# Moving the adaLN units of a three-block transformer kernel: openings of feed-forward groups, mixers that make their own gates, loads queued by free buffer

## The chip, the cores and the metric

One core of a Trainium2 chip runs the whole program. The metric is the device time of one execution in microseconds (us). TensorE (PE) multiplies, VectorE (DVE) and ScalarE (ACT) do the elementwise work, SyncE (SP) issues nearly all weight loads from one queue that is worked off in order, and GpSimd (POOL) issues a few small loads.

## The reference, cut to what matters

A sequence of 256 tokens of width 1024 passes nine sub-layers. Block 1 has two layers of feed-forward, mixer, feed-forward, each adapted by a vector c:

```python
cs = jax.nn.silu(c)
for l in range(2):
    mod = (cs @ ada_w[l] + ada_b[l]).reshape(B, 3, 3, 1024)[:, :, :, None, :]
    h = _rmsnorm(x, norm_g[l, 0]) * (1.0 + mod[:, 0, 1]) + mod[:, 0, 0]
    x = x + 0.5 * mod[:, 0, 2] * _swiglu(h, gate, up, down)
    h = _rmsnorm(x, norm_g[l, 1]) * (1.0 + mod[:, 1, 1]) + mod[:, 1, 0]
    x = x + mod[:, 1, 2] * _mixer(h, ...)
    h = _rmsnorm(x, norm_g[l, 2]) * (1.0 + mod[:, 2, 1]) + mod[:, 2, 0]
    x = x + 0.5 * mod[:, 2, 2] * _swiglu(h, gate, up, down)
return _rmsnorm(x, final_g)
```

Block 2 is one layer of feed-forward, mixer, feed-forward with norms and no adaption. The feed-forward is 2816 wide. Everything is float32.

## The kernel before

**Stages.** The nine sub-layers are stages s = 0 to 8: feed-forward, mixer, feed-forward, twice; then the same of block 2. The stage reads the normalised input `nh`/`nl` (an exact split of float32 into two parts) and ends in `change`, which adds the result to `x`, normalises it for the next stage and turns it on PE.

**Weight units.** Every weight arrives as a unit of 128 x 2048 float32 (1 MB). SP's `load(n)` puts unit n into buffer n % 3 of `raw`, after the unit three before it has been split (`lo_done`). ACT's `split` copies the unit to `hi` (rounded), DVE's `split` subtracts to get `lo` (L944), and PE multiplies three times with them. A split may start when PE is done with the unit that held the same `hi`/`lo` place: in a feed-forward four units earlier, in a mixer three. The fourth place is called `w`.

**Feed-forward.** 11 groups i = 0 to 10 of 256 hidden columns and three units each: `up(i, 0)` and `up(i, 1)` (gate and up weights, two loads for each unit) and `down(i)`. In group i PE does both halves of `up(i)` with the turning of the hidden tile of group i-1 between them, then `down(i-1)`, for which DVE's `low(i-1)` (L1086) must be done. DVE does in group i: split of `up(i+1, 0)`, `low(i-1)`, split of `up(i+1, 1)`, `mult(i)` (L1081), split of `down(i)`.

**Mixer of block 1.** Six value units (b+0 to b+5), twelve query and key units (b+6 to b+17), then four steps of three convolution units each with attention between them. Before the first of these steps PE waits until all three of its units, b+18 to b+20, are split (`arrive(c + 2)`). Then comes a tail of 18 units.

**adaLN units.** `mod` of a phase p (one phase for each of the first six stages) is 12 units of 1 MB: units 0 to 7 make scale and shift, units 8 to 11 the gate. A unit goes into `raw[:, 3]`, the one adaLN buffer, and DVE makes 256 columns of `acc` from it: `ada` is one multiply (L954) and seven multiply-adds (L957). SP's `load_ada` waits until the unit before it is used (`ada_used`); while it waits, everything behind it on SP's queue waits too. Scale and shift of phase p are due at the end of stage p-1 (`mods`), the gate of phase p in the middle of stage p (`gate_sums` on PE, `gates_in` on DVE). `ffn_ada` says which units stand behind the second `up` split of a group, ahead of `mult` (`mid`), and which behind its last split (`end`). The units stand so:

| stage | adaLN units before | after the change |
|---|---|---|
| 0 (feed-forward) | 16: phase 0 units 8 to 11, phase 1 all | 12: phase 0 units 8 to 11, phase 1 units 0 to 7 |
| 1 (mixer) | 12: phase 2 | 16: phase 1 units 8 to 11, phase 2 all |
| 2 (feed-forward) | 12: phase 3 | 9: phase 3 units 0 to 8 |
| 3 (feed-forward) | 12: phase 4 | 11: phase 3 units 9 to 11, phase 4 units 0 to 7 |
| 4 (mixer) | 12: phase 5 | 16: phase 4 units 8 to 11, phase 5 all |

In both mixers six of the units stand in the tail and do not change; the other six (before) or ten (after) stand ahead of it.

Of the kernel before, what the change touches and what calls it, by code (L numbers as in the profile page):

```python
# [43 lines left out]
NG = FF // UC  # L44
# [8 lines left out]
BASE = [sum(UNITS[k] for k in STAGES[:s]) for s in range(len(STAGES))]  # L53
# [23 lines left out]
def down_unit(i):  # L77

    return 3 * i + 4 if i < NG - 1 else 3 * NG - 1
# [32 lines left out]

def ffn_ada(s):

    if s == 0:
        units, twice = [(0, u) for u in range(8, 12)] + [(1, u) for u in range(12)], (1, 2, 3, 4, 5, 6)
    elif s in (2, 3):
        units, twice = [(s + 1, u) for u in range(12)], (3, 6)
    else:
        return [None] * NG, [None] * NG  # L120
    units = iter(units)
    mid, end = [None] * NG, [None] * NG
    for i in range(NG - 1):
        mid[i] = next(units) if i in twice else None
        end[i] = next(units)
    return mid, end


def stat_events():
# [21 lines left out]
def build(nc, a, out):  # L151
    ctx = ExitStack()
    with ctx:
# [240 lines left out]
        def _(sp):  # L394
# [13 lines left out]
            def load_ada(unit):  # L408

                if unit is None:  # L410
                    return
                p, u = unit
                n = ada_no(p, u)
                if n:
                    sp.wait_ge(ada_used, n)
                else:
                    sp.wait_ge(ada_p, 4)
                sp.dma_start(raw[:, 3, :].rearrange("p (k f) -> p k f", k=KC),
                             ada_v[p // 3][:, :, (p % 3) * 3 * D + u * UC:(p % 3) * 3 * D + (u + 1) * UC])\
                    .then_inc(raw_full[3], 16)  # L420

            def ffn(s, g_v, u_v, d_v):
                b = BASE[s]
                mid, end = ffn_ada(s)

                def up(i, kh):
                    rows_, c = slice(4 * kh, 4 * kh + 4), slice(i * UC, (i + 1) * UC)
                    load(b + up_unit(i, kh), g_v[:, rows_, c], u_v[:, rows_, c])

                up(0, 0)  # L430
                up(0, 1)
                up(1, 0)
                up(1, 1)
                load(b + down_unit(0), d_v[0])
                for i in range(NG):
                    load_ada(mid[i])
                    if i + 2 < NG:
                        up(i + 2, 0)
                        up(i + 2, 1)
                    elif i + 2 == NG:  # L440
                        load(b + down_unit(NG - 1), d_v[NG - 1])
                    load_ada(end[i])
                    if i + 2 < NG:
                        load(b + down_unit(i + 1), d_v[i + 1])

            def tail(s, at, units, srcs, wo, ada):
                for n, (kind, j) in enumerate(units):
# [7 lines left out]
            def mixer(s, l):  # L455
                b = BASE[s]
                for n in range(6):
                    e = n % 2
                    load(b + n, win_v[l][:, 4 * e:4 * e + 4, 2 * QKV + n // 2 * 512:2 * QKV + (n // 2 + 1) * 512])
                load_ada((s + 1, 0))  # L460
                for n in range(12):
                    c = n % 2 * QKV + n // 2 * UC
                    if n >= 6 and n % 2 == 0:
                        load_ada((s + 1, n // 2 - 2))
                    load(b + 6 + n, win_v[l][:, :, c:c + UC])
                for n in range(12):
                    if n in (0, 2):
                        load_ada((s + 1, 4 + n // 2))
                    c = 3 * QKV + n % 3 * D + n // 3 * UC
                    load(b + 18 + n, win_v[l][:, :, c:c + UC])  # L470
                tail(s, TAIL_AT1, TAIL1,
                     {"ga": (win_v[l], 3 * QKV + 4 * D, UC), "ya": (wao_v[l], 0, 512),
                      "gc": (win_v[l], 3 * QKV + 3 * D, UC), "yc": (wco_v[l], 0, UC)}, wo_v[l], s + 1)
# [464 lines left out]
        def _(dve):  # L938
# [21 lines left out]
            def ada(unit):  # L960
                if unit is not None:
                    ada_unit(unit[1] * UC, 3, (ada_no(*unit) + 3) * 16, ada_used)
# [87 lines left out]
                    dve.drain()  # L1050
                    V.tensor_tensor(xh, xh, f1[:, :], ALU.add).then_inc(x_done, 1)

            def change(s, early, between, behind):

                Aq = s + 1
                for t in range(2):
                    if t == 0:
                        early()
                    if s < 6:
                        add_gated(s, t)  # L1060
                    else:
                        add_postnorm(s, t)
                    if s == 5:
                        final_norm(t)
                    if s < 8:
                        normed(Aq, t)
                        if t == 0:
                            between()
                            if Aq < 6:
                                mods(Aq)  # L1070
                        apply(Aq, t)
                if s < 8:
                    behind()

            def ffn(s, fo, first=None):
                b = BASE[s]
# [20 lines left out]
                mult(0, 0)  # L1097
                mult(0, 1)
                split(b + 4)
                ada(end[0])  # L1100
                for i in range(1, NG - 1):
                    split(b + 3 * i + 2)
                    low(i - 1)
                    split(b + 3 * i + 3)
                    ada(mid[i])
                    mult(i, 0)
                    mult(i, 1)
                    if i == 6 and s < 6:
                        gates_in(s)
                    split(b + 3 * i + 4)  # L1110
                    ada(end[i])
                split(b + 32)
                low(NG - 2)
                if s < 8:
# [144 lines left out]
            def mixer(s, l):  # L1259
                b = BASE[s]  # L1260
                V.tensor_copy(cwl[:, :], vec[:, l * 24 + V_CONV:l * 24 + V_CONV + 24])
                for n in range(6):
                    split(b + n + 3)
                for r in range(6):
                    if r == 3:
                        gates_in(s)
                    split(b + 9 + 2 * r)
                    split(b + 10 + 2 * r)
                    ada((s + 1, r))
                st0 = l * STEPS  # L1270

                def conv(j, taps):
# [57 lines left out]
            def ffn_change(s, late, behind):  # L1330

                if s < 6:
                    def between():
                        late()
                        split(BASE[s + 1] + 1)
                    change(s, nothing, between, behind)
                elif s < 8:
                    def early():
                        late()
                        split(BASE[s + 1] + 1)  # L1340
                    change(s, early, nothing, behind)
                else:
                    change(s, late, nothing, nothing)

            def wo_change(s, behind):

                def between():
                    split(BASE[s + 1])
                    split(BASE[s + 1] + 1)
                change(s, nothing, between, behind)  # L1350

            for l in range(DEPTH):
                s = 3 * l
# [519 lines left out]
```

## Time and profile before

| | |
|---|---|
| median of 3 runs | 2357.85 us (2356.15 to 2358.1) |
| the profiled execution: its time, its span | 2358.23 us, 2355.8 us |
| PE busy | 2144.4 us, 91% of the span |
| DVE busy | 1428.8 us, 61% |
| ACT busy | 1008.7 us, 43% |
| read from memory | 435.05 MB, 185 GB/s over the span |

PE is the engine that is nearly always busy, so the time outside of its work is what can be won. Its idle time is the span less its busy time, 211.4 us. Where a row below has a bracket, it says how long the engine sat idle before that instruction and which engine's result ended the idle time. PEclk is the clock that TensorE was granted, as a share of full speed.

### The profile page before, as it was taken

The page shows a single profiled execution, that of the slowest core. Times are in us where ns is not written, and L with a number is a line of the kernel's source. Part 1 is how long each engine was busy: PE and PEld are TensorE (multiplying, and loading weights), DVE is VectorE, ACT ScalarE, POOL GpSimd, SP SyncE. Part 2 cuts the span into 40 slices and gives each one's busy share as a digit, 9 for nine tenths or more (in the row PEclk, how much of TensorE's full clock was granted, in tenths as well). Part 3 has the DMA queues.
Part 4 walks back from the last instruction along what each step waited for, and adds up shares of the span by engine and source line. Part 5 has one row for each costly group of instructions (what it writes and reads, how often), then busy time and mean ns, then how long its engine had stood idle before and what let it go on. Part 6 is the DMA issues. An engine that isn't in the chain of part 4 may idle for free.

```text
span 2355.8 us, 29867 instructions
## 1 busy us (share of the span) xinstructions
PE 2144.4 (91%) x12059; PEld 1860.6 (79%) x12059; DVE 1428.8 (61%) x1885; ACT 1008.7 (43%) x1249; POOL 31.3 (1%) x57
## 2 busy tenths in 40 slices
PE   6889996899989998999959999999899887799998
PEld 5677796799867776778959998887788776797887
DVE  3677645567766676766446686545544557656554
ACT  2433442443443353335324445434544546645433
POOL 0000000000000000000000000000000000000000
PEclk9999999899999999999989999999999898899999
DMA  7687565556657747766465575654555432254662
GB/s 231 222 267 247 183 210 174 154 154 203 232 171 252 249 158 245 247 227 190 159 196 136 153 253 167 213 191 146 182 193 182 140 119 72 74 193 156 213 193 90
DMA packets 355917, 438.10 MB, mean 186 GB/s; under 512 B 9563, under 2 KB 323355, under 8 KB 355780
## 3 DMA queue, kind: packets, MB, share of 16 engines
q1 hardware_dynamic: 350592, 420.51, 54.5%
q0 software_dynamic: 4160, 14.23, 2.7%
q8 instruction: 96, 1.57, 0.3%
q10 hardware_dynamic: 1028, 1.45, 0.2%
q14 instruction: 41, 0.34, 0.0%
HBM read 435.05 MB, written 1.11 MB: 185 GB/s over the span
## 4 chain that ended last, share of the span: by engine, by line
PE 54%; DVE 20%; DMA 15%; ACT 6%; issue 3%; DVEq 2%; SPq 1%; ACTq 0%
DMA raw<-in_ada_w 11%; DVE acc L957 8%; DVE lo L944 6%; PE PC L1467 4%; PE PC L1468 4%; PE PC L1469 4%; PE PA L1467 4%; PE PA L1469 4%; PE PA L1468 4%; PE PA L1460 3%; DMA raw<-in_w_in 3%; PE PA L1461 3%; PE PA L1462 3%; PE PB L1467 3%; PE PB L1469 3%; PE PB L1468 3%
## 5 line engine op out<-in xcount | busy, mean ns | idle before, releaser
L944 DVE TENSOR_TENSOR lo<-raw,hi 128x2048 fp32r<-128x2048 f32 x277 | 633.6, 2288 | 345.1 <-ACT hi L584 344.6
L584 ACT ACTIVATE hi<-raw 128x2048 fp32r<-128x2048 f32 x277 | 528.8, 1910 | 403.8 <-PE PC L1469 190.4
L1460 PE MATMUL PA<-nl,hi 128*128 128x256 f32 x976 | 291.7, 299 | 53.9 <-DVE lo L944 53.9
L1461 PE MATMUL PA<-nh,lo 128*128 128x256 f32 x976 | 284.0, 291 | 0.0
L1462 PE MATMUL PA<-nh,hi 128*128 128x256 f32 x976 | 283.2, 290 | 0.0
L957 DVE SCALAR_TENSOR_TENSOR acc<-raw,cs,acc 128x256 f32<-128x256 f32 x476 | 230.7, 485 | 36.9 <-issue 1.4
L1460 PEld LDWEIGHTS PA<-nl,hi 128*128 128x128 f32 x976 | 195.8, 201 | 56.8 <-issue 42.9
L1467 PE MATMUL PA<-hi,nl 128*128 128x512 f32 (+1 forms) x528 | 212.7, 403 | 16.2 <-DVE nl L1016 9.9
L1469 PE MATMUL PA<-hi,nh 128*128 128x512 f32 (+1 forms) x528 | 208.4, 395 | 0.0
L1468 PE MATMUL PA<-lo,nh 128*128 128x512 f32 (+1 forms) x528 | 208.1, 394 | 0.0
L1467 PE MATMUL PC<-hi,cL 128*128 128x512 f32 x384 | 160.2, 417 | 49.4 <-DVE cL L1086 44.8
L1461 PEld LDWEIGHTS PA<-nh,lo 128*128 128x128 f32 x976 | 195.7, 200 | 0.7 <-issue 0.5
L1462 PEld LDWEIGHTS PA<-nh,hi 128*128 128x128 f32 x976 | 195.3, 200 | 0.0
L1467 PE MATMUL PB<-hi,nl 128*128 128x512 f32 x400 | 158.3, 396 | 5.8 <-DVE gate_b L980 2.8
L1468 PE MATMUL PC<-lo,cH 128*128 128x512 f32 x384 | 157.0, 409 | 0.0
L1469 PE MATMUL PC<-hi,cH 128*128 128x512 f32 x384 | 156.4, 407 | 0.0
L1469 PE MATMUL PB<-hi,nh 128*128 128x512 f32 x400 | 156.1, 390 | 0.0
L1468 PE MATMUL PB<-lo,nh 128*128 128x512 f32 x400 | 155.8, 389 | 0.0
L944 DVE TENSOR_TENSOR w<-raw,w 128x2048 fp32r<-128x2048 f32 x51 | 116.6, 2287 | 36.7 <-ACT w L584 36.7
L1467 PEld LDWEIGHTS PC<-hi,cL 128*128 128x128 f32 x384 | 76.7, 200 | 75.2 <-DVE lo L944 45.0
L1467 PEld LDWEIGHTS PA<-hi,nl 128*128 128x128 f32 x528 | 102.9, 195 | 38.2 <-issue 19.1
L584 ACT ACTIVATE w<-raw 128x2048 fp32r<-128x2048 f32 x51 | 97.5, 1912 | 62.1 <-PE PC L1469 50.2
(281 smaller groups left out, 3902.4 us busy)
## 6 DMA issues: line engine op xcount, KB each, us to landing
raw<-in_w_in SPq DMA_DIRECT2D x90, 1024.0 KB, 7.2
raw<-in_ada_w SPq DMA_DIRECT2D x72, 1024.0 KB, 5.6
raw<-in_ffn_w_gate SPq DMA_DIRECT2D x88, 512.0 KB, 4.1
raw<-in_ffn_w_up SPq DMA_DIRECT2D x88, 512.0 KB, 5.3
raw<-in_ffn_w_down SPq DMA_DIRECT2D x44, 1024.0 KB, 5.6
raw<-in_ffn_w SPq DMA_DIRECT2D x88, 512.0 KB, 4.8
raw<-in_ffn_w SPq DMA_DIRECT2D x22, 1024.0 KB, 4.9
raw<-in_w_o SPq DMA_DIRECT2D x12, 1024.0 KB, 5.1
```

The lines of the kernel that those rows point to most:

```text
L584: A(parts_of(n)[0], raw[:, n % 3, :], ACT.Copy).then_inc(hi_done, 1)
L944: V.tensor_tensor(l, raw[:, n % 3, :], h.bitcast(F32), ALU.subtract).then_inc(lo_done, 1)
L957: i = V.scalar_tensor_tensor(o, w[:, k, :], cs[:, k:k + 1], o, ALU.mult, ALU.add)
L1460: MM(o, wh[:, c0:c0 + w], xl, start=first, stop=False, skip_group_check=True)
L1461: MM(o, wl[:, c0:c0 + w], xh, start=False, stop=False, skip_group_check=True)
L1462: return MM(o, wh[:, c0:c0 + w], xh, start=False, stop=last, skip_group_check=True)
L1467: MM(o, xl, wh[:, c0:c0 + w], start=first, stop=False, skip_group_check=True)
L1468: MM(o, xh, wl[:, c0:c0 + w], start=False, stop=False, skip_group_check=True)
L1469: return MM(o, xh, wh[:, c0:c0 + w], start=False, stop=last, skip_group_check=True)
```

## The change

Three things are changed at once. First, in a feed-forward the adaLN unit of group i is the first thing that DVE does in it (`ada(mid[i])`, groups 1 to 9), and the second units (`end`), of which there are three in stage 0 (groups 4, 6, 8), none in stage 2 and two in stage 3 (groups 4, 6), stand between `mult(i)` and the split of `down(i)`. Second, each mixer of block 1 makes the four gate units of its own phase, so it has ten units ahead of its tail, each behind one split. Third, SP's queue has its adaLN loads at other points: in a feed-forward behind the load of `up(i + 2, 0)`, and for the unit after a second one behind the load of `down(i + 1)`; in a mixer behind the load of b+3, and then each behind the weight load that waits for the same split as the adaLN unit before it. Besides, `low_tile` of the last hidden tile is done right after `add_gated` of the first token tile (stages 0, 2, 3, 5), and in stage 6 behind the split that it stood ahead of.

```diff
 def ffn_ada(s):
-    if s == 0:
-        units, twice = [(0, u) for u in range(8, 12)] + [(1, u) for u in range(12)], (1, 2, 3, 4, 5, 6)
-    elif s in (2, 3):
-        units, twice = [(s + 1, u) for u in range(12)], (3, 6)
-    else:
+    phases = {0: (0, 8, 1, 8), 2: (3, 0, 3, 9), 3: (3, 9, 4, 8)}
+    if s not in phases:
         return [None] * NG, [None] * NG
+    p0, u0, p1, u1 = phases[s]
+    units = [(p0, u) for u in range(u0, 12 if p1 > p0 else u1)] + [(p1, u) for u in range(u1 if p1 > p0 else 0)]
+    twice = (4, 6, 8)[:len(units) - 9]
...
+    for i in range(1, NG - 1):
+        mid[i] = next(units)
+        end[i] = next(units) if i in twice else None
+MIX_ADA = (1, 3, 5, 6, 8, 10, 11, 13, 15, 17)
+def mix_ada(s):
+    return [(s, u) for u in range(8, 12)] + [(s + 1, u) for u in range(6)]
 # SP, feed-forward
-                for i in range(NG):
-                    load_ada(mid[i])
-                    if i + 2 < NG:
-                        up(i + 2, 0)
-                        up(i + 2, 1)
-                    elif i + 2 == NG:
-                        load(b + down_unit(NG - 1), d_v[NG - 1])
-                    load_ada(end[i])
-                    if i + 2 < NG:
-                        load(b + down_unit(i + 1), d_v[i + 1])
+                for i in range(NG - 2):
+                    up(i + 2, 0)
+                    load_ada(end[i] or mid[i + 1])
+                    up(i + 2, 1)
+                    load(b + down_unit(i + 1), d_v[i + 1])
+                    if end[i]:
+                        load_ada(mid[i + 1])
+                load(b + down_unit(NG - 1), d_v[NG - 1])
 # SP, mixer
-                load_ada((s + 1, 0))
+                    if n == 3:
+                        load_ada(mix_ada(s)[0])
                 for n in range(12):
-                    if n >= 6 and n % 2 == 0:
-                        load_ada((s + 1, n // 2 - 2))
                     load(b + 6 + n, win_v[l][:, :, c:c + UC])
+                    if n in MIX_ADA:
+                        load_ada(mix_ada(s)[MIX_ADA.index(n) + 1])
                 for n in range(12):
-                    if n in (0, 2):
-                        load_ada((s + 1, 4 + n // 2))
                     load(b + 18 + n, win_v[l][:, :, c:c + UC])
+                    if n + 12 in MIX_ADA[:-1]:
+                        load_ada(mix_ada(s)[MIX_ADA.index(n + 12) + 1])
 # DVE, change
                         add_postnorm(s, t)
+                    if t == 0:
+                        midway()
 # DVE, feed-forward
-                ada(end[0])
                 for i in range(1, NG - 1):
+                    ada(mid[i])
                     split(b + 3 * i + 2)
                     low(i - 1)
                     split(b + 3 * i + 3)
-                    ada(mid[i])
                     mult(i, 0)
                     mult(i, 1)
                     if i == 6 and s < 6:
                         gates_in(s)
+                    ada(end[i])
                     split(b + 3 * i + 4)
-                    ada(end[i])
 # DVE, mixer
-                for n in range(6):
+                for n in range(18):
+                    if n == 12:
+                        gates_in(s)
                     split(b + n + 3)
-                for r in range(6):
-                    if r == 3:
-                        gates_in(s)
-                    split(b + 9 + 2 * r)
-                    split(b + 10 + 2 * r)
-                    ada((s + 1, r))
+                    if n in MIX_ADA:
+                        ada(mix_ada(s)[MIX_ADA.index(n)])
 # DVE, ffn_change (late is low_tile of the last hidden tile)
                 if s < 6:
-                    def between():
-                        late()
-                        split(BASE[s + 1] + 1)
-                    change(s, nothing, between, behind)
+                    change(s, nothing, late, lambda: split(BASE[s + 1] + 1), behind)
                 elif s < 8:
                     def early():
+                        split(BASE[s + 1] + 1)
                         late()
-                        split(BASE[s + 1] + 1)
-                    change(s, early, nothing, behind)
+                    change(s, early, nothing, nothing, behind)
```

## Rows read from the trace of the kernel before

**Rows 1.** The page: the chain that ended last, by engine.
```profile
PE 54%; DVE 20%; DMA 15%; ACT 6%; issue 3%; DVEq 2%; SPq 1%; ACTq 0%
```

**Rows 2.** Windows: busy us of PE, PEld, DVE, ACT, POOL; PEclk, DMA share, GB/s.
```profile
96.00:101.00 5.00, 4.97 (x12) 3.96 (x13) 4.38 (x6) 0.00 (x0) 0.00 (x0) 0.52 1.08 354
...
330.00:421.00 91.00, 63.85 (x504) 62.08 (x502) 45.41 (x54) 27.87 (x23) 0.00 (x0) 0.89 0.57 182
```

**Rows 3.** Timeline of PE, stages 1 and 4: start us, us, instruction, idle before.
```profile
370.26 0.38 PE L1460 MATMUL PC<-nl,hi 128*128 128x256 f32 x1 [1.69 <-DVE lo L944]
...
421.24 0.55 PE L1460 MATMUL PA<-nl,hi 128*128 128x256 f32 x1 [21.08 <-DVE lo L944]
...
1223.95 0.55 PE L1460 MATMUL PA<-nl,hi 128*128 128x256 f32 x1 [20.96 <-DVE lo L944]
```

**Rows 4.** Timelines of SP, ACT and DVE, one period of stage 1.
```profile
374.41 0.37 SPq L418 DMA_DIRECT2D raw<-in_ada_w  x1
374.82 1.89 SPq L406 DMA_DIRECT2D raw<-in_w_in  x2
...
382.60 1.91 ACT L584 ACTIVATE hi<-raw 128x2048 fp32r<-128x2048 f32 x1 [11.32 <-DMA raw<-in_w_in]
...
384.55 2.29 DVE L944 TENSOR_TENSOR lo<-raw,hi 128x2048 fp32r<-128x2048 f32 x1 [6.76 <-ACT hi L584]
387.18 3.84 DVE L957 SCALAR_TENSOR_TENSOR acc<-raw,cs,acc 128x256 f32<-128x256 f32 x7
```

**Rows 5.** Timeline of ACT: evictions of query and key units, PE never idle.
```profile
326.59 0.60 ACT L812 ACTIVATE q<-PA 128x512 f32<-128x512 f32 x1 [2.87 <-PE PA L1462]
...
332.35 0.60 ACT L810 ACTIVATE k<-PA 128x512 f32<-128x512 f32 x1 [3.37 <-PE PA L1462]
```

**Rows 6.** Timeline of DVE, stage 6: `low` of two groups with no adaLN unit.
```profile
1713.37 0.69 DVE L1086 TENSOR_TENSOR cL<-PA,cH 128x512 fp32r<-128x512 f32 x1 [2.38 <-ACT cH L671]
...
1730.23 0.69 DVE L1086 TENSOR_TENSOR cL<-PB,cH 128x512 fp32r<-128x512 f32 x1 [2.40 <-ACT cH L671]
```

**Rows 7.** Timelines of SP and DVE: first burst of stage 2; of stage 3.
```profile
664.46 0.37 SPq L406 DMA_DIRECT2D raw<-in_ffn_w_gate  x1
...
667.62 0.51 SPq L418 DMA_DIRECT2D raw<-in_ada_w  x1
...
676.48 0.35 DVE L954 TENSOR_SCALAR acc<-raw,cs 128x256 f32<-128x256 f32 x1 [6.98 <-DMA raw<-in_ada_w]
...
880.61 0.37 SPq L406 DMA_DIRECT2D raw<-in_ffn_w_gate  x1
```

**Rows 8.** Timeline of ACT, stage 2: the second `up` unit of that burst.
```profile
673.48 1.92 ACT L584 ACTIVATE hi<-raw 128x2048 fp32r<-128x2048 f32 x1 [1.20 <-DMA raw<-in_ffn_w_up]
```

**Rows 9.** Timelines of SP and DVE, stage 0: an adaLN load with little ahead of it.
```profile
93.11 0.37 SPq L418 DMA_DIRECT2D raw<-in_ada_w  x1
...
98.36 0.35 DVE L954 TENSOR_SCALAR acc<-raw,cs 128x256 f32<-128x256 f32 x1 [0.28 <-DMA raw<-in_ada_w]
```

**Rows 10.** PE: first `down`, gate sums, ninth `down` of stage 0; ninth, stages 2, 3.
```profile
96.03 0.77 PE L1467 MATMUL PC<-hi,cL 128*128 128x512 f32 x1 [7.59 <-DVE cL L1086]
...
194.18 1.98 PE L1519 MATMUL PB<-acc,ones_w 128*128 128x512 f32 x4 [3.03 <-DVE cL L1086]
...
250.05 0.47 PE L1467 MATMUL PC<-hi,cL 128*128 128x512 f32 x1 [2.03 <-DVE cL L1086]
...
832.51 0.47 PE L1467 MATMUL PC<-hi,cL 128*128 128x512 f32 x1 [0.99 <-DVE cL L1086]
...
1051.74 0.47 PE L1467 MATMUL PC<-hi,cL 128*128 128x512 f32 x1 [1.84 <-DVE cL L1086]
```

**Rows 11.** Timelines of DVE and PE at the end of stage 5.
```profile
1651.74 1.13 DVE L1008 TENSOR_SCALAR ub_b<-PC,vec 128x128 f32<-128x128 f32 x4 [4.09 <-PE PC L1529]
...
1645.60 0.77 PE L1467 MATMUL PC<-hi,cL 128*128 128x512 f32 x1 [4.54 <-DVE cL L1091]
```

**Rows 12.** Timeline of DVE, the end of stage 6.
```profile
1842.46 0.42 DVE L1091 TENSOR_TENSOR cL<-PA,cH 128x256 fp32r<-128x256 f32 x1 [3.81 <-ACT cH L675]
```

More of the change, by code:

```diff
@@ L113, in ffn_ada @@
 def ffn_ada(s):
-    if s == 0:
-        units, twice = [(0, u) for u in range(8, 12)] + [(1, u) for u in range(12)], (1, 2, 3, 4, 5, 6)
-    elif s in (2, 3):
-        units, twice = [(s + 1, u) for u in range(12)], (3, 6)
-    else:
+    phases = {0: (0, 8, 1, 8), 2: (3, 0, 3, 9), 3: (3, 9, 4, 8)}
+    if s not in phases:
         return [None] * NG, [None] * NG
+    p0, u0, p1, u1 = phases[s]
+    units = [(p0, u) for u in range(u0, 12 if p1 > p0 else u1)] + [(p1, u) for u in range(u1 if p1 > p0 else 0)]
+    twice = (4, 6, 8)[:len(units) - 9]
     units = iter(units)
     mid, end = [None] * NG, [None] * NG
-    for i in range(NG - 1):
-        mid[i] = next(units) if i in twice else None
-        end[i] = next(units)
+    for i in range(1, NG - 1):
+        mid[i] = next(units)
+        end[i] = next(units) if i in twice else None
     return mid, end
+MIX_ADA = (1, 3, 5, 6, 8, 10, 11, 13, 15, 17)
+def mix_ada(s):
+    return [(s, u) for u in range(8, 12)] + [(s + 1, u) for u in range(6)]
 def stat_events():
@@ L1051, in add_postnorm, with change @@
                     V.tensor_tensor(xh, xh, f1[:, :], ALU.add).then_inc(x_done, 1)
-            def change(s, early, between, behind):
+            def change(s, early, midway, between, behind):
                 Aq = s + 1
@@ L1332, in ffn_change @@
                 if s < 6:
-                    def between():
-                        late()
-                        split(BASE[s + 1] + 1)
-                    change(s, nothing, between, behind)
+                    change(s, nothing, late, lambda: split(BASE[s + 1] + 1), behind)
                 elif s < 8:
                     def early():
+                        split(BASE[s + 1] + 1)
                         late()
-                        split(BASE[s + 1] + 1)
-                    change(s, early, nothing, behind)
+                    change(s, early, nothing, nothing, behind)
                 else:
-                    change(s, late, nothing, nothing)
+                    change(s, late, nothing, nothing, nothing)
             def wo_change(s, behind):
@@ L1349, in between @@
                     split(BASE[s + 1] + 1)
-                change(s, nothing, between, behind)
+                change(s, nothing, nothing, between, behind)
             for l in range(DEPTH):
```

## The prediction

> **What bounds the kernel now.** I read the page's chain of waits first: PE holds 54% of it, but DVE 20% and transfers 15% [rows 1], so there are stretches in which PE is not what sets the time. The list of PE's gaps then says where. The largest are alike: 21.08 us in stage 1 and 20.96 us in stage 4, both ahead of the first convolution unit, both ended by a DVE split [rows 3]. The window ahead of the first shows PE busy 63.9 of 91 us, with the transfers at 182 GB/s, far from the 354 GB/s that another window reaches [rows 2]. So neither PE nor the memory is full there; a loop of waits is. One turn of it is seen in [rows 4]: SP issues an adaLN load and two weight loads together, ACT waits for the weight unit until 382.60 (8.2 us after the first issue), its split takes 1.91, DVE's 2.29, the adaLN unit 0.35 + 3.84 = 4.2, and only then may SP issue again, 16.6 us for two units. PE needs 332.35 - 326.59 = 5.76 us a unit [rows 5], 11.5 for two.
>
> The feed-forwards that carry adaLN units have a weaker form of it. A group without them takes 1730.23 - 1713.37 = 16.86 us [rows 6], all of it PE's. In stage 0 the ninth `down` starts 250.05 - 96.03 = 154.0 us after the first [rows 10]; eight groups and the gate sums (1.98) would be 136.9.
>
> **The mixers: two times -24.7.** The loads: SP now waits for a used adaLN buffer only at the point where the next weight load would wait for a later split anyway, so the loop of [rows 4] is cut. What is left is PE's pace. Unit b+14 started at 370.26 after 1.69 idle [rows 3], so without a wait at 368.6. Four units to the end of b+17 give 368.6 + 4 x 5.76 = 391.6. The split of b+20 cannot start before that: eviction 0.60, ACT 1.91, DVE 2.29 make 396.4, and PE starts the convolution there. Before it started at 421.24: 24.8 us. The second mixer has the same gap, so two make 49.5. The clock after either gap is taken as the same: a wait of 4.5 to 21 us stands there both times.
>
> The four gate units more cost DVE 4 x 4.2 = 16.8 us a mixer. DVE has 18 splits of 2.3 and ten adaLN units of 4.2, 83 of some 100 us, so they lie beside PE's work, provided that the units land in time. The condition: from the unit behind the split of b+8 (begun near 326: PE ends b+5 at 391.6 - 12 x 5.76 - 2.0 = 320.5, then 1.1 eviction by my estimate from two of 0.55, 1.91, 2.29) to the one behind the split of b+18 there are six more, each a landing L and 4.2, then two splits, 4.6. 330.2 + 6(L + 4.2) + 4.6 stays under 396.4 for L up to 6.1. An adaLN load with one or two older loads nearly done landed in 98.36 - 93.11 = 5.25 us [rows 9]; here one weight load is issued 4.2 us ahead of each, so I take 5.3 to 6 and no cost. Every us of L above 6.1 costs 6 us a mixer. Bounds: 0 at 5.25; at 8.9, the last of a burst of three (676.48 - 667.62, [rows 7]), 17 us a mixer. The bytes: 28 MB units in 100 us are 294 GB/s, against 354 seen.
>
> **Feed-forward groups with one unit: a gain.** The adaLN load is now second behind `up(i + 2, 0)`. The second unit of such a burst was there 673.48 - 664.46 = 9.0 us after the first issue [rows 7, 8]. DVE's turn is then 9.0 + 4.2 + 2.3 = 15.5 us, under PE's 16.86, so these groups run at PE's pace; before, the load stood third and the turn was longer. At a stage's start the first unit lands at 673.5 instead of 676.48 and PE's first `down` comes 3.0 us sooner.
>
> **Stage 2: -12.9.** All nine units are single. First `down` at 673.5 + 4.2 + 2.3 + 0.7 = 680.7, eight groups 134.9, gate sums 2.0, and 2.0 for the clock after the first wait: ninth `down` at 819.6, before 832.51 [rows 10]. The clock term: after 7.59 us idle PE ran five us at a granted 0.52, the lower level (1.2 GHz), [rows 2, 10], which loses 2.2 to 2.4; after a shorter wait between 0 and that, I take 2.0.
>
> **Groups with two units: a loss of 10.3 each, five of them.** Count from the start g of PE's group. The first unit is done near g + 3.3, the split of `up(i + 1, 0)` at 5.6. Then the second unit's load goes out behind `up(i + 2, 0)` and is there 9.0 later, 14.6; the unit is done at 18.8, the split of `down(i)` at 21.1. Only now SP may pass on to the load of `down(i + 1)` and the next adaLN load behind it, and DVE has that unit as the first thing of its next group: everything on DVE is queued behind this wait, the split of `up(i + 2, 0)` and `low(i)` too. Two loads issued together took 382.60 - 374.41 = 8.2 [rows 4]: 29.3, unit 33.5, split 35.8, `low` 36.5. PE wants `low(i)` after two thirds of its next group, at 16.9 + 11.3 = 28.2. It waits 8.3 us, and 2.0 go to the clock. The group after it runs at PE's pace again and wins no more than is needed to repeat this. Bounds of one: with both landings 5.25 the wait is 1.7 and the clock term goes; with both 12.0 (676.48 - 664.46) it is 14.8 and 2.
>
> **Stage 0: +12.7.** From first to ninth `down` 136.9 + 2.0 + 3 x 10.3 = 169.8 against 154.0, with a start 3.1 sooner. **Stage 3: +4.6.** Before, its ninth `down` is 1051.74 - 832.51 = 219.2 behind that of stage 2 and its start 880.61 - 664.46 = 216.2, so it was 3.1 slower; now it is as stage 2 with 2 x 10.3: -12.9 - 3.1 + 20.6.
>
> **The ends of stages.** Stage 5: `low_tile` held up PE's last `down` for 4.54 us [rows 11] because two statistics of ACT stood before it. It moves into DVE's wait for the first of them. What follows is held by DVE's wait of 4.09 for the turned tile [rows 11], of which the split ahead of it does not let more go: -4.1 (bounds 0 and -6.6, the wait with the clock). Stage 6: the split now fills the 3.81 us in which DVE waited for ACT [rows 12]; next is ACT's statistics: -0.7 of at most 2.3. In stages 0, 2 and 3 PE is at `mods` and the turning meanwhile: 0, and 0.4 each either way if that cover were gone. The orders of stages 7 and 8 and of the opening stay.
>
> **Sum.** -49.5 - 12.9 + 12.7 + 4.6 - 4.1 - 0.7 = -49.9. The profiled execution took 2358.2 (span 2355.8 and 2.4 around it): 2308.3. The median of the runs is 0.4 below it, so **2308**.
>
> **Rivals.**
> *Cheaper doubled groups (0.13), 2286.* The older load may be nearly through when the adaLN load follows, as where 5.25 us were measured [rows 9]. Against it: it is issued under 1 us ahead. Halfway to that bound five groups give back 5 x 4.3 = 22.
> The Trainium skill, page "DMA: Bandwidth & Descriptors", section "Anatomy of one DMA — SWDGE (gpsimd) path", puts a DMA at 2.0 us and its bytes at 436 GB/s (for GpSimd's queue; these loads are SP's). Two loads at once would then be here in an estimated 6.8 us, a doubled group 3.6 us cheaper, the sum near 2290. By the rows it is too fast: a single load comes to 4.4 by it and took 5.25 [rows 9].
> *The mixers' loads land late (0.15), 2333.* Value units and bias tiles crowd the transfers and L is 8.2 as in [rows 4]: 6 x 2.1 = 12.6 us a mixer, 25 in all.
> *Slower than before (0.06), 2379.* The same loop with adaLN loads third behind two weight loads, L = 12.0 [rows 7]: 6 x 5.9 = 35 a mixer. It decides from L = 10.3, where 12 x 4.2 eat the 50. For it speaks that DVE holds a finished load back behind nothing but itself; against it that older loads are 4.2 us gone.
> *It does not do what it says (0.04), 2358.* PE's gap of 21 us stays since DVE blocks on the adaLN unit instead of SP. That needs DVE to idle 20 us more than counted.
>
> **How the numbers follow.** The forecast case has 0.60, with a range of its own of 2294 to 2322 (doubled groups 7.5 to 13 each, mixers 0 to 8 late together). The range over the cases is 2284 to 2334. What a measurement of this kernel tells from no change is about 0.2%. Faster 0.90, within it 0.03, slower 0.07; what is left over, 0.02, is split.
>
> **What would show it.** PE's gap ahead of L1460 in the mixers falls from 21 us to about 4.8. Stage 2 has no wait of PE for `low` after the first. PE waits 7 to 11 us for `low` five times, in groups 5, 7 and 9 of stage 0 and 5 and 7 of stage 3, and DVE waits for an adaLN transfer right ahead of each. The gap at the end of stage 5 is gone. I am wrong if the doubled groups cost under 5 or over 15 us, or if DVE's waits for adaLN transfers in the mixers exceed 4 us each.

## The result, and the profile after

The changed kernel takes 2299.8 us (median; 2298.8 to 2301.31) against 2357.97 for the kernel before on the same chip: a ratio of 0.9754, 95% interval 0.9737 to 0.9771. The forecast was 2308, in a range of 2284 to 2334: the result lies in the range, 8 us below the point. The profiled execution has a span of 2297.2 us, 58.6 less than before.

The page of the changed kernel: busy time of the engines, and the chain that ended last.

```profile
PE 2134.2 (93%) x12059; PEld 1857.3 (81%) x12059; DVE 1433.7 (62%) x1885; ACT 1008.7 (44%) x1249; POOL 31.4 (1%) x57
...
PE 70%; DVE 14%; DMA 6%; ACT 6%; issue 2%; DVEq 2%; SPq 1%; ACTq 0%
```

In the chain DVE's share fell from 20 to 14% and that of transfers from 15 to 6% [rows 1], and PE holds what they gave up. The list of waits says where the rest still sits (what waits, for what; us in all, times, longest):

```profile
DVE acc L961 <- DMA raw<-in_ada_w: 103.3, 32, 8.0
...
PE PC L1470 <- DVE cL L1095: 51.0, 8, 8.9
```

Eight waits of PE for `low`, 51 us in all. The timeline of PE shows them, and the gap ahead of the convolution in each mixer:

```profile
92.37 0.47 PE L1470 MATMUL PC<-hi,cL 128*128 128x512 f32 x1 [3.99 <-DVE cL L1095]
...
169.15 0.76 PE L1470 MATMUL PC<-hi,cL 128*128 128x512 f32 x1 [7.50 <-DVE cL L1095]
...
214.88 0.77 PE L1470 MATMUL PC<-hi,cL 128*128 128x512 f32 x1 [8.75 <-DVE cL L1095]
...
259.97 0.76 PE L1470 MATMUL PC<-hi,cL 128*128 128x512 f32 x1 [8.87 <-DVE cL L1095]
...
407.06 0.36 PE L1463 MATMUL PA<-nl,hi 128*128 128x256 f32 x1 [4.86 <-issue]
...
666.06 0.47 PE L1470 MATMUL PC<-hi,cL 128*128 128x512 f32 x1 [4.14 <-DVE cL L1095]
...
867.71 0.47 PE L1470 MATMUL PC<-hi,cL 128*128 128x512 f32 x1 [4.03 <-DVE cL L1095]
...
944.34 0.77 PE L1470 MATMUL PC<-hi,cL 128*128 128x512 f32 x1 [7.38 <-DVE cL L1095]
...
989.13 0.76 PE L1470 MATMUL PC<-hi,cL 128*128 128x512 f32 x1 [6.36 <-DVE cL L1095]
...
1169.93 0.55 PE L1463 MATMUL PA<-nl,hi 128*128 128x256 f32 x1 [4.86 <-issue]
```

The gaps of 21.08 and 20.96 us [rows 3] are 4.86 each. Three waits of 7.5 to 8.9 us in stage 0 and two of 6.4 and 7.4 in stage 3 are new: one behind each group with two adaLN units. The other three stand at the first `down` of stages 0, 2 and 3.

For the lengths of the stages I take the first product that PE does on the second token tile at each stage's start, one row per stage in either trace (76.70, 303.91, 644.11, 845.87, 1066.80, 1406.61 and 1594.53 after). Us:

| stage | before | after | difference | forecast |
|---|---|---|---|---|
| 0, feed-forward, 12 units in 9 groups | 216.6 | 227.2 | +10.6 | +12.7 |
| 1, mixer | 365.1 | 340.2 | -24.9 | -24.7 |
| 2, feed-forward, 9 units | 216.1 | 201.8 | -14.4 | -12.9 |
| 3, feed-forward, 11 units | 220.5 | 220.9 | +0.4 | +4.6 |
| 4, mixer | 365.9 | 339.8 | -26.0 | -24.7 |
| 5 | 192.7 | 187.9 | -4.8 | -4.1 |
| 6 to 8 | 702.3 | 702.7 | +0.4 | -0.7 |

In the mixers the window ahead of the convolution (busy us of PE, PEld, DVE, ACT, POOL; granted clock, DMA share, GB/s) is the counterpart of the second of [rows 2]:

```profile
330.00:407.00 77.00, 72.21 (x587) 70.81 (x585) 58.33 (x73) 32.95 (x28) 0.00 (x0) 1.00 0.90 288
```

PE is busy for 94% of it at full clock, where it was 70%; the transfers run at 288 GB/s (182 before; the prediction estimated 294). Timelines of SP and DVE there, two adaLN loads:

```profile
340.85 0.37 SPq L426 DMA_DIRECT2D raw<-in_ada_w  x1
...
369.23 0.37 SPq L426 DMA_DIRECT2D raw<-in_ada_w  x1
...
346.04 0.35 DVE L961 TENSOR_SCALAR acc<-raw,cs 128x256 f32<-128x256 f32 x1 [3.02 <-DMA raw<-in_ada_w]
...
375.15 0.35 DVE L961 TENSOR_SCALAR acc<-raw,cs 128x256 f32<-128x256 f32 x1 [3.74 <-DMA raw<-in_ada_w]
```

These two land 5.2 and 5.9 us after their issue. Of the other seven of stage 1, six took 5.1 to 5.5 us and one 6.5, for which DVE did not wait. In the mean they stay under the 6.1 from which the prediction said that they would cost. DVE waits for three of the ten units of stage 1, 3.74 us at most.

### The profile page after: what moved, and what is told of

Its sections match the earlier page's. It is cut to its first block, busy times and chain, and to the rows that moved or that the text cites. A ratio compares the mean times of both kernels' runs of the same rounds, so it can differ in the third digit from the quotient of the medians.

```text
span 2297.2 us, 29867 instructions
## 1 busy us (share of the span) xinstructions
PE 2134.2 (93%) x12059; PEld 1857.3 (81%) x12059; DVE 1433.7 (62%) x1885; ACT 1008.7 (44%) x1249; POOL 31.4 (1%) x57
## 4 chain that ended last, share of the span: by engine, by line
PE 70%; DVE 14%; DMA 6%; ACT 6%; issue 2%; DVEq 2%; SPq 1%; ACTq 0%
DMA raw<-in_ada_w 6%; PE PC L1470 5%; PE PC L1472 5%; PE PC L1471 5%; PE PA L1470 5%; PE PA L1472 5%; PE PA L1471 5%; DVE lo L951 5%; PE PA L1463 5%; PE PA L1464 4%; PE PA L1465 4%; PE PB L1470 4%; PE PB L1472 4%; PE PB L1471 4%; DVE acc L964 4%
## 5 line engine op out<-in xcount | busy, mean ns | idle before, releaser
L1463 PEld LDWEIGHTS PA<-nl,hi 128*128 128x128 f32 x976 | 195.7, 201 | 16.8 <-issue 10.5
L1472 PEld LDWEIGHTS PA<-hi,nh 128*128 128x128 f32 x528 | 102.2, 194 | 21.1
```

The lines of the kernel that those rows point to most:

```text
L1463: MM(o, wh[:, c0:c0 + w], xl, start=first, stop=False, skip_group_check=True)
L1472: return MM(o, xh, wh[:, c0:c0 + w], start=False, stop=last, skip_group_check=True)
```

## The experiments

All eight kernels compute the whole reference. The first four ran on one chip (kernel before: 2356.08, 2352.39 to 2357.25), the last four on another (2356.71, 2352.76 to 2360.15).

| kernel | median us | ratio to before, 95% interval | span |
|---|---|---|---|
| mix_order | 2305.88 | 0.9786 (0.9772 to 0.9801) | 2301.7 |
| mid_first | 2271.84 | 0.9644 (0.9629 to 0.9658) | 2267.3 |
| end_first | 2278.45 | 0.9670 (0.9654 to 0.9686) | 2276.4 |
| both_first | 2241.01 | 0.9510 (0.9495 to 0.9524) | 2239.0 |
| low_late | 2305.14 | 0.9784 (0.9769 to 0.9799) | 2302.1 |
| old_ffn_order | 2300.79 | 0.9760 (0.9743 to 0.9778) | 2299.4 |
| old_counts | 2264.21 | 0.9608 (0.9592 to 0.9624) | 2262.4 |
| mixer_load_late | 2386.73 | 1.0129 (1.0114 to 1.0144) | 2385.8 |

### mix_order: only the place of the mixers' loads

The kernel before, with nothing changed but where SP queues five of the six adaLN loads that a mixer has ahead of its tail (the first stays where it was):

```diff
                 for n in range(12):
-                    if n >= 6 and n % 2 == 0:
-                        load_ada((s + 1, n // 2 - 2))
                     load(b + 6 + n, win_v[l][:, :, c:c + UC])
+                    if n >= 6 and n % 2:
+                        load_ada((s + 1, n // 2 - 2))
                 for n in range(12):
-                    if n in (0, 2):
-                        load_ada((s + 1, 4 + n // 2))
                     load(b + 18 + n, win_v[l][:, :, c:c + UC])
+                    if n in (1, 3):
+                        load_ada((s + 1, 4 + n // 2))
```

> The kernel before, with one change: in the two mixers of block 1 each of the six adaLN loads ahead of the tail is queued behind the weight load that waits for the same split as the adaLN unit before it. Units, their counts and DVE's order are as before. My theory (SP's queue closed a loop of waits): PE's gap of 21 us ahead of the first convolution unit falls to about 5 us in both mixers, stages 1 and 4 get 24 to 26 us shorter each, the other stages stay, the time is about 2307 us. Rival (the gain came from DVE's new order, one adaLN unit behind every other split with ten of them spread over the stage): the gaps stay near 21 us and the time near 2357 us.

Measured: 2305.88. Both mixers take 339.9 us, as long as in the changed kernel (340.2 and 339.8). PE's timeline has the same gap as there:

```profile
396.33 0.55 PE L1460 MATMUL PA<-nl,hi 128*128 128x256 f32 x1 [4.86 <-issue]
```

So the whole gain of the mixers, 51 us of the 58, is the queue's order, with DVE's order left as it was. That the changed kernel makes four more units there (16.8 us of DVE) costs nothing beside it.

### mid_first, end_first, both_first: an adaLN load ahead of the weight load it was issued with

In the first, after a second unit the next adaLN load goes ahead of that of `down(i + 1)`; in the second, the adaLN load of each group goes ahead of `up(i + 2, 0)`; the third does both.

```diff
                 for i in range(NG - 2):
+                    load_ada(end[i] or mid[i + 1])       # end_first, both_first
                     up(i + 2, 0)
-                    load_ada(end[i] or mid[i + 1])       # end_first, both_first
                     up(i + 2, 1)
-                    load(b + down_unit(i + 1), d_v[i + 1])  # mid_first, both_first
                     if end[i]:
                         load_ada(mid[i + 1])
+                    load(b + down_unit(i + 1), d_v[i + 1])  # mid_first, both_first
```

> The changed kernel, with one change in the feed-forwards: behind a second unit of a group the load of the next group's adaLN unit is queued ahead of the load of down(i + 1), not behind it. My theory (the five waits of PE of 6.4 to 8.9 us come from that load being held by the split of down(i) and landing behind another load): the unit lands about 5 us sooner, each of the five waits falls by 4.5 to 5.5 us, with the clock about 2275 us (2268 to 2282). Rival (DVE has too much to do in these groups, two units of 4.2 us and three splits, the loads don't matter): the waits fall by under 1.5 us each, 2293 to 2300 us.

> The changed kernel, with one change in the feed-forwards: the adaLN load of each group is queued ahead of the load of up(i + 2, 0), not behind it. My theory: it goes out as soon as its buffer is free and lands in 5 to 6 us instead of 9, so PE's first wait of stages 0, 2 and 3 falls from 4.0 to about 0.5 us and the second unit of a doubled group costs 2 to 2.5 us less; groups with one unit, which are PE's already, don't change: 2275 to 2287 us, point 2280. Rival (up(i + 2, 0) is then late and holds PE, since it now stands behind 1 MB more): new waits of PE for a split of up, 2300 us or more.

> The changed kernel with both of these orders of the queue. My theory: a doubled group's two units are each ready when DVE comes to them, PE's wait falls to 0 to 2 us and the clock does not drop, so that stages 0, 2 and 3 come to 200 to 206 us each: 2246 us (2238 to 2256). Rival (DVE's work of 17.6 us in a doubled group against PE's 16.9 and the transfers of 5 MB in it set a floor): doubled groups keep 3 us or more each, 2262 us or more.

Measured: 2271.84, 2278.45 and 2241.01, each in its range and below its point. In end_first the first wait of stage 0 fell only to 2.20 us, where about 0.5 was expected; in stages 2 and 3 it is 0.47 and 0.48. The two loads together gain 58.8 us on the changed kernel, more than the 28.0 and 21.4 of each alone; why the two add up to more was not tried. This is the first of the doubled groups of stage 0 in the changed kernel, timelines of SP and DVE:

```profile
138.96 0.37 SPq L414 DMA_DIRECT2D raw<-in_ffn_w_gate  x1
...
139.92 0.51 SPq L426 DMA_DIRECT2D raw<-in_ada_w  x1
...
154.04 0.37 SPq L414 DMA_DIRECT2D raw<-in_ffn_w_down  x1
154.45 0.47 SPq L426 DMA_DIRECT2D raw<-in_ada_w  x1
...
147.54 0.35 DVE L961 TENSOR_SCALAR acc<-raw,cs 128x256 f32<-128x256 f32 x1 [1.84 <-DMA raw<-in_ada_w]
...
161.93 0.35 DVE L961 TENSOR_SCALAR acc<-raw,cs 128x256 f32<-128x256 f32 x1 [7.92 <-DMA raw<-in_ada_w]
...
168.32 0.68 DVE L1095 TENSOR_TENSOR cL<-PA,cH 128x512 fp32r<-128x512 f32 x1
```

And its like in both_first:

```profile
146.47 0.37 SPq L426 DMA_DIRECT2D raw<-in_ada_w  x1
148.67 0.37 SPq L414 DMA_DIRECT2D raw<-in_ffn_w_down  x1
...
151.48 0.35 DVE L961 TENSOR_SCALAR acc<-raw,cs 128x256 f32<-128x256 f32 x1 [2.84 <-DMA raw<-in_ada_w]
...
155.66 2.28 DVE L951 TENSOR_TENSOR lo<-raw,hi 128x2048 fp32r<-128x2048 f32 x1
157.86 0.68 DVE L1095 TENSOR_TENSOR cL<-PA,cH 128x512 fp32r<-128x512 f32 x1
...
158.69 0.47 PE L1470 MATMUL PC<-hi,cL 128*128 128x512 f32 x1 [0.48 <-DVE cL L1095]
```

The chain is: the load's issue, its landing, DVE's work on the unit (4.2), the split (2.29), `low`. With the weight load ahead, the adaLN unit starts 7.9 us after the pair's first issue (154.04 to 161.93); ahead of it, 5.0 after its own (146.47 to 151.48). The `down` unit, now issued second, costs PE nothing: in stage 0 of both_first, PE's only waits above 0.3 us between the first and the ninth `down` are those for `low`. `low` stands at 157.86 instead of 168.32, and PE's wait is 0.48 instead of 7.50. The five waits of PE are 7.50, 8.75, 8.87, 7.38, 6.36 in the changed kernel; 2.69, 3.65, 4.46, 2.55, 2.43 with the one load moved; 5.42, 7.18, 5.52, 5.51, 5.92 with the other; and 0.48, 1.09, 0.66, 0.66, 1.05 with both. Stages 0, 2 and 3 are then 195.1, 196.8 and 200.3 us, two of them shorter than the 200 to 206 expected. From their first `down` to their ninth they take 139.5, 136.6 and 138.9 us with three, no and two doubled groups, so a doubled group still costs 1.0 to 1.2 us. This version is 4.9% faster than the kernel before and, by the two ratios (0.9510 / 0.9754 = 0.975), some 2.5% faster than the changed one.

### low_late: the third part undone

`low_tile` stands again where it stood in the kernel before.

```diff
-                    change(s, nothing, late, lambda: split(BASE[s + 1] + 1), behind)
+                    def between():
+                        late()
+                        split(BASE[s + 1] + 1)
+                    change(s, nothing, nothing, between, behind)
```

(and in stage 6 `late()` ahead of the split.)

> The changed kernel with its smallest part undone: low_tile of the last hidden tile stands where it stood before, at the ends of stages 0, 2, 3, 5 and 6. My theory: PE's wait of 4.5 us ahead of its last down of stage 5 is back and stage 5 is 4 to 5 us longer, stage 6 by 0.7, the rest the same: 2304.5 us where the changed kernel has 2299.8. Rival (that wait is hidden behind the statistics anyway): under 1 us, 2300.

Measured: 2305.14. Stage 5 is 192.7 us again and PE's wait is back:

```profile
1591.45 0.76 PE L1473 MATMUL PC<-hi,cL 128*128 128x512 f32 x1 [4.53 <-DVE cL L1100]
```

What the move does in the time is stage 5's 4.8 us. Stages 6 to 8 take 702.4 us in it, against 702.7 in the changed kernel, which tells nothing of the 0.7 expected in stage 6: the seven kernels with the changed order there take from 700.4 to 703.0 for these stages. The waits themselves do tell, see stage 6 below.

### old_ffn_order: the new counts in the old order

The changed kernel, with the feed-forwards' order on SP and DVE as before (units at the ends of groups 0 to 9, of 0 to 8 in stage 2; second ones in groups 3 and 6 of stage 0 and in group 3 of stage 3). The core of it:

```diff
-                for i in range(NG - 2):
-                    up(i + 2, 0)
-                    load_ada(end[i] or mid[i + 1])
-                    up(i + 2, 1)
-                    load(b + down_unit(i + 1), d_v[i + 1])
-                    if end[i]:
-                        load_ada(mid[i + 1])
+                for i in range(NG):
+                    load_ada(mid[i])
+                    if i + 2 < NG:
+                        up(i + 2, 0)
+                        up(i + 2, 1)
...
+                    load_ada(end[i])
+                    if i + 2 < NG:
+                        load(b + down_unit(i + 1), d_v[i + 1])
```

> The changed kernel, its counts of adaLN units in each stage kept (12, 16, 9, 11, 16) and its mixers too, but with the order of before inside the feed-forwards, on DVE and on SP's queue (second units in groups 3 and 6, or 3 alone). My theory (stage 2 is won by the order, at a count of one unit a group): stage 2 goes back to 214 to 218 us from 201.8 though it has three units fewer than before; stage 0 gets shorter, to 212 to 216 from 227, since it loses the doubled groups' waits; stage 3 about 218 to 220; in all 2298 us (2292 to 2304). Rival (fewer units are what pays): stage 2 stays at 202 to 206 and the time falls under 2290.

Measured: 2300.79 (2295.3 to 2302.28), which cannot be told from the changed kernel's 2299.8. Stages 0, 2 and 3 are 215.7, 219.3 and 218.1 us, against 227.2, 201.8 and 220.9. Stage 2, with nine units in the old order, is even longer than the 216.1 of the kernel before with twelve (and 1.3 above the range expected), so it was not the smaller count that won it. The run puts back DVE's order and SP's together; which of the two wins stage 2 was not parted. The new order, as it came, gains 17.5 us in the stage with single units and gives back 11.5 and 2.8 in the two with doubled groups. Taken alone it is worth about nothing; with the two swaps of both_first it is worth about 60 (2300.8 - 2241.0).

### old_counts: the old counts in the best order

both_first, but with 16, 12 and 12 units in stages 0, 2 and 3 and six in each mixer:

```diff
-    phases = {0: (0, 8, 1, 8), 2: (3, 0, 3, 9), 3: (3, 9, 4, 8)}
+    phases = {0: (0, 8, 1, 12), 2: (3, 0, 3, 12), 3: (4, 0, 4, 12)}
...
-    twice = (4, 6, 8)[:len(units) - 9]
+    twice = (4, 6, 8) if s else (1, 2, 3, 4, 5, 6, 7)
...
-MIX_ADA = (1, 3, 5, 6, 8, 10, 11, 13, 15, 17)
+MIX_ADA = (7, 9, 11, 13, 15, 17)
```

> The orders of both_first, on DVE and on SP's queue, with the counts of before: 16, 12, 12, 12, 12 units, mixers that leave their gates to the feed-forward ahead of them. Thirteen doubled groups instead of five. My theory (with the loads in time a doubled group costs PE about 1 us and DVE 0.7 more than PE's 16.9): the mixers stay at 340 us, stages 0, 2 and 3 grow by 6 to 14 us in all: 2250 us (2246 to 2257) beside 2241. Rival (the gates in the mixers are what frees the feed-forwards): over 2265 us.

Measured: 2264.21, above the range and just under the rival's 2265. Stage 0 took 213.4 us instead of 195.1, stages 2 and 3 took 201.8 and 199.8 (196.8 and 200.3). I had priced a doubled group by itself; in stage 0 seven of them follow each other. Timelines of SP and DVE over one of them, and PE's rows at the start of the second and fourth `down`:

```profile
97.02 0.37 SPq L426 DMA_DIRECT2D raw<-in_ada_w  x1
...
106.39 0.37 SPq L426 DMA_DIRECT2D raw<-in_ada_w  x1
...
116.25 0.37 SPq L426 DMA_DIRECT2D raw<-in_ada_w  x1
...
102.08 0.35 DVE L961 TENSOR_SCALAR acc<-raw,cs 128x256 f32<-128x256 f32 x1 [2.89 <-DMA raw<-in_ada_w]
...
111.94 0.35 DVE L961 TENSOR_SCALAR acc<-raw,cs 128x256 f32<-128x256 f32 x1
...
122.34 0.35 DVE L961 TENSOR_SCALAR acc<-raw,cs 128x256 f32<-128x256 f32 x1 [3.91 <-DMA raw<-in_ada_w]
...
109.31 0.58 PE L1470 MATMUL PC<-w,cL 128*128 128x512 f32 x1 [2.17 <-DVE cL L1095]
...
149.33 0.47 PE L1470 MATMUL PC<-hi,cL 128*128 128x512 f32 x1 [2.65 <-DVE cL L1095]
```

A turn is: landing 5.1, unit 4.2, then two splits, a `low` and `mult` (5.7 to the start of the next unit), unit 4.2. That is 116.25 - 97.02 = 19.2 us, and two groups of PE take 149.33 - 109.31 = 40.0 where 33.7 would be its own. In both_first, where a single group follows each doubled one, PE's wait comes to 1.09 at most; with seven in a row, each turn adds to the delay. So the new counts are worth some 23 us (2264.2 - 2241.0): 18.3 of it in stage 0 and 5.0 in stage 2, where one adaLN load took 7.0 us to land (704.33 to 711.38) and PE waited 2.87 us behind that doubled group; its like in stage 3 took 5.1, and PE waited 0.64.

### mixer_load_late: the price of a late load

The changed kernel with nine of the ten adaLN loads that a mixer has ahead of its tail (all but the first) one weight load later:

```diff
-                    if n in MIX_ADA:
-                        load_ada(mix_ada(s)[MIX_ADA.index(n) + 1])
+                    if n - 1 in MIX_ADA:
+                        load_ada(mix_ada(s)[MIX_ADA.index(n - 1) + 1])
```

(and the same for b+18 to b+29.)

> The changed kernel, with the adaLN loads of the mixers ahead of the tail queued behind one weight load more, so that each leaves 2.3 us later and right behind 1 MB. This is the rival of my prediction that ended on the slower side, made on purpose. By its price (a landing counted from the unit before of 10.5 us, against 6.1 that is free, six times a mixer) each mixer is 26 us longer: 2352 us (2335 to 2360), near the kernel before. Other theory (the spread over ten units leaves DVE enough time to absorb the landing): the mixers grow by under 8 us each, 2300 to 2315 us.

Measured: 2386.73, 1.3% slower than before. The direction was right, the size was not: +87 us on the changed kernel where I expected about 52. Stages 1 and 4 grew by 41.3 and 46.9. Timelines of SP and DVE:

```profile
336.30 0.58 SPq L426 DMA_DIRECT2D raw<-in_ada_w  x1
...
314.80 0.35 DVE L961 TENSOR_SCALAR acc<-raw,cs 128x256 f32<-128x256 f32 x1
...
329.38 0.35 DVE L961 TENSOR_SCALAR acc<-raw,cs 128x256 f32<-128x256 f32 x1 [3.62 <-DMA raw<-in_ada_w]
...
344.20 0.35 DVE L961 TENSOR_SCALAR acc<-raw,cs 128x256 f32<-128x256 f32 x1 [6.14 <-DMA raw<-in_ada_w]
...
450.21 0.35 DVE L961 TENSOR_SCALAR acc<-raw,cs 128x256 f32<-128x256 f32 x1 [5.98 <-DMA raw<-in_ada_w]
```

DVE's timeline of the changed kernel, the first and the tenth unit:

```profile
314.81 0.35 DVE L961 TENSOR_SCALAR acc<-raw,cs 128x256 f32<-128x256 f32 x1
...
406.88 0.35 DVE L961 TENSOR_SCALAR acc<-raw,cs 128x256 f32<-128x256 f32 x1
```

Look at one turn. A unit ends 4.2 after its start, at 333.6; the next load goes out at 336.30, behind a split and a weight load, and is there at 344.20. So L is 10.6, and a turn 14.8 with the unit. From the first unit's start to the tenth's the nine turns take 450.21 - 314.80 = 135.4 us, 14.6 to 16.8 each. In the changed kernel they take 406.88 - 314.81 = 92.1, which is PE's pace, 16 units of 5.76 or 92.2. The difference, 43.3, is near what stage 1 lost (41.3). In stage 4 the nine turns take 140.6 (five of the nine loads took 8.9 to 9.4 us to land there; in stage 1 one took 9.8 and the others 7.6 to 7.9) and the stage lost 46.9. The expected L of 10.5 was right; what was wrong is the number of turns: the loop binds over all nine, not over the six that I counted behind b+8. With nine it would have been 9 x 14.7 - 92.2 = 40.1 a mixer.

## Why the prediction was right, point by point

**The mixers (-24.7 each): right, mechanism and size.** Measured are -24.9 and -26.0, and the gap is 4.86 as forecast. That the order of the loads alone does it is shown by mix_order; that the four more units lie beside PE is shown by the equal length of its stages. The condition, L up to 6.1, came out right though it was derived from six turns: with the nine turns that mixer_load_late showed, 9 (L + 4.2) = 92.2 gives 6.0, and the landings are 5.4 us in the mean in stage 1 and 5.6 in stage 4. Single ones above it (6.5, and 7.2 in stage 4) cost nothing as the others make up for them: the nine turns add up to 92.1 us in either stage, PE's own pace.

**The price beyond it (6 us for each us of L): too low.** It is nine, one for each turn. The step that failed is the count of turns that bind. It did not enter the sum, but two rivals rested on it: loads late by 8.2 would have cost 9 x 12.4 - 92.2 = 19.4 a mixer instead of 12.6, and the slower case would have begun near L = 8.8 (9 x 13.0 - 92.2 = 25), not 10.3. The mixers were nearer to a loss than I wrote.

**Feed-forward with single units (-12.9): right.** Stage 2 gained 14.4. The first `down` waits 4.14 us, and behind it stands no wait for `low`. From the first `down` to the ninth the stage takes 138.2 us, forecast were 138.9; the first `down` comes 3.4 us sooner, forecast were 3.0. That the order does it and not the count is shown by old_ffn_order.

**Doubled groups (+10.3 each, five of them): right in place, order and size.** PE waits in groups 5, 7 and 9 of stage 0 and 5 and 7 of stage 3, behind DVE's wait for the adaLN transfer. What one costs in all is read against stage 2 of the same kernel, which has none, from the first `down` to the tenth. (The slow clock behind the third doubled group of stage 0 falls into the time between ninth and tenth.) The tenth `down` of stages 0, 2 and 3 on PE's timeline:

```profile
278.85 0.40 PE L1470 MATMUL PC<-w,cL 128*128 128x512 f32 x1
...
821.12 0.40 PE L1470 MATMUL PC<-w,cL 128*128 128x512 f32 x1
...
1042.28 0.40 PE L1470 MATMUL PC<-w,cL 128*128 128x512 f32 x1
```

With the first ones at 92.37, 666.06 and 867.71 this makes 186.5, 155.1 and 174.6 us. So three doubled groups cost 31.4 in stage 0 and two cost 19.5 in stage 3, 10.2 each in the mean. Of this 7.8 is the wait (8.3 forecast; the landings were 8.6, from 138.96 to 147.54, and 7.9 where the prediction had 9.0 and 8.2) and 2.4 comes behind it (2.0 forecast, for the clock). In the five us behind each of the five waits the granted clock is 0.72, 0.51, 0.59, 0.50 and 0.50, with PE busy throughout, so it is wholly or for the most part the lower level (1.2 GHz). This is the fourth:

```profile
944.34:949.34 5.00, 5.00 (x12) 3.95 (x13) 4.92 (x4) 0.00 (x0) 0.00 (x0) 0.50 0.96 292
```

The bounds that the prediction gave for the wait of one were a little off: from its own landings 5.25 each gives 1.6 and 12.0 each gives 15.1, not 1.7 and 14.8. Nothing rested on it.

**Where the sum was too small by 8.7 us (58.6 measured, 49.9 forecast).** One term was missing: the sum looked at stages 0 and 3 only up to the ninth `down`. The kernel before lost time behind it too. Its tenth ones on PE's timeline:

```profile
268.60 0.40 PE L1467 MATMUL PC<-w,cL 128*128 128x512 f32 x1
...
1070.28 0.40 PE L1467 MATMUL PC<-w,cL 128*128 128x512 f32 x1
```

They stand 18.5 us behind the ninth ones (250.05 and 1051.74), where a group of PE's own takes 16.8. The changed kernel had 18.9 in stage 0, which is the clock counted above, and 16.8 in stage 3. So 1.7 us in each of the two stages were free to be won and not in the sum, 3.4 in all. The mixers gave 1.4 more than forecast. The eight groups behind the first `down` took 0.7 less in each of the three stages, by the measure of stage 2, or 2.0 in all. The first `down` came 3.4 to 3.6 us sooner instead of 3.0 to 3.1, 1.3 in all. Stage 5 gave 0.7 more, the doubled groups cost 0.6 less, and stages 6 to 8 gave 1.1 less. This leaves 0.4 in no one place. That the point lies within 8.2 us of the result is thus no luck of large errors that cancel: all but one of the differences have the same sign, and none is above 3.4.

**Rival "cheaper doubled groups", 2286: not seen.** It had each of them 4.3 us cheaper; they were 0.1 cheaper. The Trainium skill, page "DMA: Bandwidth & Descriptors", section "Anatomy of one DMA — SWDGE (gpsimd) path", gives an estimated 6.8 us for two 1 MiB loads issued together and 4.4 for one. Here, from SP's queue, 7.9 and 5.0 were measured: the traces do not agree in the size, and agree roughly in the step that the older load adds, 2.4 us by the page and 2.9 here.

**Rivals of the mixers: not seen.** Late loads (L = 8.2) did not come, though mixer_load_late shows that moving the loads by one place makes a kernel of 2387 us out of it, above the 2379 of the slower rival. "Does not do what it says" fell with the gap.

**Stage 5 (-4.1): right,** -4.8, shown by low_late. **Stage 6 (-0.7): right in the wait, not seen in the time.** Every wait of DVE went as told: behind `low_tile`, ACT's statistics are next, 1.39 us. PE's wait for the tile that it turns became 0.71 shorter. But then PE turned the tile at a lower clock. PE's timeline of the changed kernel, and its window of that row:

```profile
1789.83 1.97 PE L1532 MATMUL PC<-ident,xn_a 128*128 128x128 f32 x8 [2.14 <-DVE xn_a L1004]
```

```profile
1789.80:1791.80 2.00, 1.97 (x8) 1.57 (x8) 0.37 (x1) 0.82 (x3) 0.00 (x0) 0.52 0.00 0
```

The same two of the kernel before:

```profile
1850.40 1.09 PE L1529 MATMUL PC<-ident,xn_a 128*128 128x128 f32 x8 [2.85 <-DVE xn_a L997]
```

```profile
1850.40:1851.50 1.10, 1.09 (x8) 0.85 (x8) 0.33 (x1) 0.41 (x2) 0.00 (x0) 1.00 0.00 0
```

The wait became 0.71 shorter and the turning 0.88 longer, at a granted 0.52 instead of 1.00. The wait is 2.13 to 2.14 us in all seven kernels with the new place of `low_tile` and 2.85 to 2.86 in all three with the old one (before, mix_order, low_late). Behind the longer wait the turning took 1.09 in all three. Behind the shorter it took 1.09 in mid_first, both_first and old_ffn_order and 1.8 to 2.0 in the other four, which takes back what the move wins there. What decides it stays open.

## What to carry to other kernels

Where one in-order queue feeds two consumers, look for the load whose buffer comes free last, and for everything queued behind it: moving five loads in each mixer behind two more weight loads was worth 51 us, and moving nine of ten one weight load further cost 87. Of two loads that are issued together, the one whose landing heads the longer chain goes first: two such swaps were worth 59 us here. Price a loop by all its turns, from the first that binds: one doubled group with single ones around it cost about 1 us, but when seven follow each other their own period shows, 19.2 us against PE's 16.9. And follow a stage to its end when the gain is summed up: what the old kernel loses behind the last point looked at is missing from the sum.

## What the runs showed of the hardware

How long a load takes depends on what was issued just ahead of it. From SP's queue a 1 MiB adaLN load was there 5.0 us after its issue where the loads ahead of it were 5 us old (both_first, 146.47), and 5.1 to 5.9 in stage 1 of the changed kernel, but for one of 6.5. Behind a weight load issued 0.4 us before, it was there 7.9 us after the pair's first issue (7.5 after its own), and 8.6 behind a weight load in two pieces (7.6 after its own). So with 288 GB/s moving in the mixers the landing hardly grew, and one load issued just ahead added 2.5 us to it, 2.9 counted from the first issue.

The granted clock after a wait depends on more than the wait: about 2.14 us ahead of the same turning was followed by 0.52 in the changed kernel and by a turning of full speed in both_first, mid_first and old_ffn_order.
